# Clearing a DRAM buffer from ScalarE's queue instead of SyncE's, and two more filler matmuls, in a two-layer transformer kernel

## What is computed

```
y_lat = finish(o_lat)                         # (rmsnorm(o) * gain) @ w_out
h_lat = h_lat + gt_ml * y_lat
f_lat = modulate(rmsnorm(h_lat, g_ffn[layer]), sh_fl, sc_fl)
scores = sigmoid(f @ w_router);  biased = scores + b_router
top_idx = top 8 of the 64 experts, within the best 4 of 8 groups
routed[token] = sum over its 8 experts of w * (silu(f @ w_gate[e]) * (f @ w_up[e])) @ w_down[e]
```

## Time and profile before

| what | value |
|---|---|
| time, three runs | 2601.9, 2603.1 and 2611.2 us; median 2603.1 us |
| profiled execution | its own time 2611.2 us, span 2609.4 us |
| busy share of the span | TensorE 90%, VectorE 32%, ScalarE 26%, GpSimd 10% |
| mean granted TensorE clock | 0.96 of full speed |
| stage out(0) ends, moe(0) starts | 617.6 us from the span's start |
| stage out(1) | 1837 to 1931 us |
| moe(1) | 1931 us to the end |

### The profile page before, as it was taken

One profiled execution on the slowest core, in us unless ns is written; L12 is line 12 of the kernel. 1 busy time (PEld: TensorE's weight loads), 2 busy tenths in 40 slices (PEclk: granted clock), 3 DMA queues, 4 the chain that ended last, 5 costly groups with the idle time before them and its releaser, 6 DMA issues. The chain is left out here.

```text
span 2609.4 us, 34210 instructions
## 1 busy us (share of the span) xinstructions
PE 2357.6 (90%) x13502; PEld 1248.8 (48%) x13502; DVE 838.3 (32%) x1740; ACT 665.4 (26%) x1443; POOL 273.8 (10%) x257
## 2 busy tenths in 40 slices
PE   7999999798899999999994779998879998888888
PEld 3544555475544333333331768886645332333333
DVE  2332556626610100001013955555363110000006
ACT  1111444521012121211212344445311121111111
POOL 1000000032011111111111000000111111111100
PEclk8999999998999999999997899999989999999999
DMA  8566200212479999999995711110848999999996
GB/s 331 191 227 201 109 1 1 70 65 78 188 293 351 377 394 386 390 374 383 381 340 209 271 45 38 37 31 1 329 171 313 414 419 419 419 419 409 415 369 283
DMA packets 125998, 661.90 MB, mean 254 GB/s; under 512 B 18692, under 2 KB 29956, under 8 KB 64145
## 3 DMA queue, kind: packets, MB, share of 16 engines
q1 hardware_dynamic: 97024, 574.04, 56.3%
q0 software_dynamic: 28816, 85.69, 8.4%
HBM read 604.38 MB, written 72.96 MB: 260 GB/s over the span
## 5 line engine op out<-in xcount | busy, mean ns | idle before, releaser
L1622 PE MATMUL E_psG<-E_gu,E_xT 128*32 128x512 f32 (+2 forms) x2544 | 528.0, 609 | 48.0 <-DMA E_gu<-in_we_up_dram 32.9
L1956 DVE TENSOR_TENSOR E_hh<-E_sil,E_psG 128x256 f32<-128x256 f32 x96 | 40.4, 421 | 1078.8 <-ACT E_sil L1784 1078.8
L1622 PEld LDWEIGHTS E_psG<-E_gu,E_xT 128*32 128x32 f32 (+2 forms) x2544 | 156.8, 121 | 289.8 <-issue 282.8
L1636 PE MATMUL E_psY<-E_dn,E_hT 128*32 128x512 f32 (+2 forms) x1272 | 261.9, 596 | 1.5 <-ACT E_hT L1787 1.5
L1622 PE MATMUL E_psG<-fT,E_xT 128*32 128x512 f32 (+2 forms) x704 | 236.6, 618 | 3.7 <-DMA E_gu<-in_we_up_dram 3.2
L1622 PE MATMUL E_psG<-o,E_xT 128*32 128x512 f32 (+2 forms) x736 | 224.2, 610 | 5.7 <-DMA E_gu<-in_we_up_dram 5.7
L1784 ACT ACTIVATE E_sil<-E_psG 128x256 f32<-128x256 f32 x96 | 36.9, 384 | 657.7 <-PE E_psG L1622 657.7
L1497 POOL DMA_INDIRECT y_d<-E_yb,E_sca x91 | 91.6, 1007 | 950.9 <-ACT E_yb L1790 950.9
L1790 ACT ACTIVATE E_yb<-E_psY,E_wgt 128x1024 f32<-128x1024 f32 x95 | 105.9, 1115 | 285.7 <-PE E_psY L1636 285.7
L1622 PE MATMUL E_psG<-raw,E_xT 128*32 128x512 f32 (+2 forms) x464 | 148.4, 594 | 1.2 <-DVE E_xT L1953 1.2
L150 PE MATMUL I_psC<-I_w_hi,I_aT_hi 128*128 128x384 f32 (+1 forms) x336 | 111.2, 331 | 20.2 <-DVE I_aT_lo L2297 16.6
(11 more groups left out here) (452 smaller groups left out, 3757.9 us busy)
## 6 DMA issues: line engine op xcount, KB each, us to landing
E_gu<-in_we_gate_dram SPq DMA_DIRECT2D x70, 1024.0 KB, 4.9
E_gu<-in_we_up_dram SPq DMA_DIRECT2D x70, 1024.0 KB, 6.8
E_dn<-in_we_down_dram SPq DMA_DIRECT2D x70, 1024.0 KB, 7.1
h<-in_w_ada_dram SPq DMA_DIRECT2D x40, 1024.0 KB, 4.8
o<-in_we_gate_dram SPq DMA_DIRECT2D x24, 1024.0 KB
o<-in_we_up_dram SPq DMA_DIRECT2D x24, 1024.0 KB
o<-in_we_down_dram SPq DMA_DIRECT2D x24, 1024.0 KB
I_ring<-y_d SPq DMA_DIRECT2D x24, 1024.0 KB, 7.0
```

The lines of the kernel that those rows point to most:

```text
L1622: ins = nc.tensor.matmul(psG[c:c + n, 0].rearrange("p (v f) -> p v f", v=2), xT[:, k, c:c + n], slots[s][0][:, :, k], start=(k == 0), stop ...
L1636: ins = nc.tensor.matmul(psY[c:c + w, n], hT[:, j, k, c:c + w], slots[s][1][:, k, n * 512:(n + 1) * 512], start=(k == 0), stop=(k == KF - 1))
L1956: V.tensor_tensor(hh[:], sil[:], psG[:, 0, FF:2 * FF], ALU.mult).then_inc(done, 1)
```

## The change

Three edits in `stage_out`. The eight clears, with the wait on the zero tile ahead of them, go from SyncE's list to ScalarE's, behind the splits of the weights and ahead of the loop over tiles. The wait for their landing goes from the end of SyncE's list to the end of ScalarE's. `stay_busy` runs 7 matmuls in both layers instead of 5 in layer 0 and 7 in layer 1.

```diff
                         sp.dma_start(w_r[:], kview(a["w_router"][l])).then_inc(s_wr, 16)
-                        if clear:
-                            sp.wait_ge(s_zt, 1)
-                            for c in range(clear_rows.shape[0]):
-                                sp.dma_start(clear_rows[c], zero[:].unsqueeze(1).to_broadcast([P, TOPK // 2, D])).then_inc(s_z, 16)
                         for t in range(nt):
...
                         for b in range(2):
                             sp.wait_ge(s_fd[b], 16 * ((nt - b + 1) // 2))
-                        if clear:
-                            sp.wait_ge(s_z, 16 * clear_rows.shape[0])
...
                         for k in range(KD):
                             act.wait_ge(s_w[k], 16)
                             nc.scalar.activation(w_hi[:, k], w_raw[k], ACT.Copy).then_inc(s_wh, 1)
+                        if clear:
+                            act.wait_ge(s_zt, 1)
+                            for c in range(clear_rows.shape[0]):
+                                act.dma_start(clear_rows[c], zero[:].unsqueeze(1).to_broadcast([P, TOPK // 2, D])).then_inc(s_z, 16)
                         for t in range(nt + 1):
...
                         nc.scalar.activation(su[:, 1, 0], psY[:, 0, FF:2 * FF], ACT.Copy)
+                        if clear:
+                            act.wait_ge(s_z, 16 * clear_rows.shape[0])
...
-                        stay_busy(psT[:, (n - 1) % 2, 0:4].rearrange("p k n -> p (k n)"), 5 if nt > NL else 7)
+                        stay_busy(psT[:, (n - 1) % 2, 0:4].rearrange("p k n -> p (k n)"), 7)
```

## The result

The changed kernel took 2628.8 us (median of 4, 2626.5 to 2629.4) against 2603.9 us of the kernel before: ratio 1.0089, 95% interval 1.0068 to 1.0109, so slower by 17.7 to 28.4 us. The forecast was 2624 us. Both say slower; the size is known only to about 10 us by timing, and the output stage's share of it better by the profiles.

A forecast was written before the change was run, and what follows sets the result against it. The prediction took the kernel to be bound by a chain through the second output stage, whose end moves the kernel's end equally. +23.5 + 2.9 - 3.3 - 2 = +21.1 us on 2603.1 gave 2624 us, range 2615 to 2632.

The forecast's parts named there:

- ScalarE's stall: Second output stage: eight issues hold ScalarE until about 1878.9, delaying evac, low(1), y of tile 0, product of tile 1; +23.5 us.
- The restart at the low clock: TensorE's product of tile 1, second output stage: after the stop, fifteen matmuls start at the slow distance; +2.9 us.
- What comes back on SyncE's side: Second output stage: stores of f no longer behind clears, shared product neither waits nor runs slow; -3.3 us, at most 4.1.
- The longer filler: stay_busy 5 to 7, first output stage: costs nothing, may speed the next stage's ranks; 0 or 4.5 to 6, taken -2 us.
- The sum: Whole kernel: +23.5 + 2.9 - 3.3 - 2 = +21.1 us on the median of 2603.1, giving 2624 us.

The follow-up runs named there:

- e_act_spread: Changed kernel with the eight clears spread over ScalarE's list (three behind the splits, the rest behind the norms of tiles 0 to 2); ratio to before 0.9971.
- e_act_behind: Changed kernel with all eight clears one step further down ScalarE's list, behind evac of tile 1; ratio to the kernel before 1.0037.
- e_wide2: Changed kernel with an 8 KB instead of 4 KB zero tile per partition, same bytes in half as many pieces; ratio to the kernel before 1.0019.
- e_sp_spread: Kernel before with stay_busy 7 and the clears left on SyncE but spread among the stores of f; 2599.6 us, ratio 0.9964.
- e_early_clear: Changed kernel with the clears issued by SyncE in the first attention stage, none in the output stage; 2598.0 us, ratio to before 0.9948.
- e_stay7: Kernel before with only stay_busy changed in the first output stage, 7 matmuls instead of 5; ratio 1.0001.
- e_stay2: Kernel before with 2 filler matmuls instead of 5 in the first output stage; ratio 0.9998.
- the two timings: Changed kernel against the kernel before, timed first (2628.8 against 2603.9 us, ratio 1.0089) and again beside a control (2623.4 against 2608.8 us, ratio 1.0049).
- e_act_clear: Kernel before with only the clears moved to ScalarE's list, stay_busy left as it was; ratio 1.0102.

## Why the prediction was right, and where it was off

**ScalarE's stall: right.** Its queue behaves as SyncE's. The eighth issue was forecast to end at 1878.9 in the time of the profile before; there the mix stage ends 8.6 us later than in the profile after, so the measured 1869.5 is 1878.1. TensorE's product of tile 1 came 22.7 us later in its stage (23.44 us of waiting instead of 0.70), forecast 23.5. e_act_spread, e_act_behind and e_wide2 show that it is the draining and the order behind it: same engine, same bytes, and 88, 105 and 104 us of stage against 115 in the changed kernel. The Trainium skill ("DMA: Bandwidth & Descriptors", Issuing engines are not separate DMA queues) is right that the transfers themselves don't care who starts them, as the three placements of e_act_spread, e_sp_spread and e_early_clear show within 1 us; that issuing is usually small holds for 6.2 us in e_act_spread and not for 27.4 us here.

**The restart at the low clock: right, somewhat too large.** 2.9 us forecast. Eleven matmuls started 0.43 us apart from 1874.03 on, where 2.4 GHz gives 0.23: 2.1 us. The fifteen of the forecast were those of one other restart, in one profile; at that same restart e_stay7 has about half as many.

**What comes back on SyncE's side: too small.** I added what TensorE shows in front of and in the shared product, 2.39 us of waiting and 1.75 us of slow clock, and took 3.3 us of it, at most 4.1. The stages without the trouble are 5.9 us (e_sp_spread, whose shared product is slow) to 6.8 us shorter than before. What the step had wrong is the path: the late store sets the time at which TensorE can start the shared product, and the wait in front of it is only what TensorE had not already lost on the way. The shared product starts 74.6 to 74.8 us into the stage in all five profiles with the eight clears in one go on SyncE, and after 68.9 to 69.9 us in the three other placements. That is about 5 to 6 us, and where the shared product then runs at 2.4 GHz 1.75 us more.

Before, 1.9 us of it lie in two places that I left out: the 0.56 us wait of the transposes for f and a stretch at the low clock at the start of the last product, seven matmuls from 1890.7 on (1.3 us):

```profile
1891.31 0.63 PE L1232 MATMUL D_psY<-D_wl,D_oTh 128*128 128x512 f32 x1
1891.74 0.63 PE L1233 MATMUL D_psY<-D_wh,D_oTl 128*128 128x512 f32 x1
```

That stretch is no price of the store by itself, and where it comes from stays open. e_stay7 and e_stay2 have the same late store and no such stretch; TensorE waits 3.2 and 3.0 us for f instead, and the shared product starts at the same time. In e_stay7, whose stage counts from 1832.75:

```profile
1900.71 1.16 PE L1214 MATMUL D_psT<-cst,D_f 128*128 128x128 f32 x8 [3.21 <-POOL D_f L1198]
...
1907.33 9.40 PE L1240 MATMUL D_psY<-o,fT 128*128 128x512 f32 x16 [0.68 <-DVE D_y L1171]
```

In the changed kernel itself the shared product stayed slow (8.78 us) although its wait was gone, so nothing of the 1.75 us came back. From the product of tile 1 to the shared product are 48.9 us instead of 51.5, and 2.1 us of them are the restart, so 4.8 us came back there. That makes 22.7 + 2.1 - 4.8 = 20.0 us, the measured growth of the stage (the third term is taken from the difference), where the forecast had 23.1.

**The longer filler: right in the rows, not seen in the time.** I took -2 us, either 0 or 4.5 to 6. In the profiles it is all or nothing, as forecast: the head takes 27.3 to 28.5 us or 21.5 to 21.8. All eight profiles with 7 fillers have the short one, and two of four with 5. That would be 3 to 4 us on the mean. But that the longer filler costs nothing holds only where the clock stays high in it. In four of the eight (both profiles of the changed kernel among them) the fourteen records take 7.92 us instead of 6.23, and the next stage begins 2.55 us after VectorE's last instruction instead of 1.17, so 1.4 us are lost again. The timings of e_stay7 and e_stay2 (each within 0.17% of before) neither show nor exclude the 2 to 3 us that are left. The clock did not do what I said, though: I had it fall in the middle of the ranks, 1.8 us later than before, while in all eight profiles it didn't fall during them.

**The sum.** 21.1 us forecast; by the profiles' pieces 20.0 in the output stage less 0 to 7 in the head; by the two timings 24.9 and 14.5 us between medians. The forecast change lies inside the first interval (17.7 to 28.4) and above the second (8 to 17). That the second median, 2623.4 us, is the forecast 2624 almost to the digit is luck: the kernel before took 2608.8 us beside it, and not the 2603.1 from which I counted. The direction, and that it is the stall on ScalarE, is shown; the size of the whole is not, to better than about 10 us. The better version was at hand: the three placements here that put no more than three of these transfers ahead of something urgent are 0.3 to 0.5% faster than the kernel before (with the longer filler in all three, which alone gave a ratio of 1.0001).

## What to carry to other kernels

Before a DMA moves to an engine that also computes, read how long its issues take where they are: here issues whose time equalled bytes over bandwidth meant a full queue, and whatever followed on the new engine stood that time out. Then ask how much is queued at once, and not for which engine. Against the stage with the clears spread (88.3 us), the same 16 MB in one go cost 26.6 us on ScalarE and 6.6 us on SyncE. What a late store costs is read from when it lets the waiting engine go on, and not from the length of the last wait: lost time ahead of that wait, such as a stretch at the low clock, hides in it.

## What the runs showed of the hardware that was not expected

- ScalarE's queue took more bytes ahead when the same bytes came in larger pieces: by the trace's packets 7.1 MB were still to move at the end of the last issue where the clears make 4224 packets, and 11.8 MB where they make 2176.
- 42 rank matmuls keep TensorE busy from start to end, yet where the clock was low ahead of them it stayed low through all of them (9.2 us, in before, e_act_clear and e_stay2), and where it was high it stayed high for their 4.87 us.
